# Squares behind the high parts, a raw tile of its own for the third down chunk, and block sums and squares moved into pass two, in a one-core decoder layer

## The reference

```python
def reference(x, ..., mlp_pre_g, w_up, w_down, mlp_post_g):
    ...
        h = h + rms_norm(mix @ w_out[l], attn_post_g[l])
        u = rms_norm(h, mlp_pre_g[l])
        a = jnp.square(jax.nn.relu(u @ w_up[l]))       # 1024 -> 4096
        h = h + rms_norm(a @ w_down[l], mlp_post_g[l]) # 4096 -> 1024
    return h
```

## Time and profile before

| what | value |
|---|---|
| median of 3 runs | 611.48 us (611.33 to 612.48) |
| the profiled execution's own time | 612.76 us |
| its span in the trace | 611.0 us |
| TensorE busy (matmuls) | 580.5 us, 95% |
| VectorE busy | 410.3 us, 67% |
| ScalarE busy | 310.6 us, 51% |
| GpSimd busy | 108.8 us, 18% |
| mean DMA rate | 166 GB/s |
| up stage, chunk 2 to the last | 276.57 to 440.83 us of the span |
| down product | 440.83 to 603.66 us |

### The profile page before, as it was taken

The page is one execution under the profiler, slowest core; times in us unless marked ns, Lnnn a source line. Parts: engine busy times, 40 slices in busy tenths (PEclk is TensorE's granted clock), DMA queues, the critical chain, the costliest instruction groups (busy, mean ns, idle before and its releaser), DMA issues.

```text
span 611.0 us, 8355 instructions
## 1 busy us (share of the span) xinstructions
PE 580.5 (95%) x2900; PEld 483.4 (79%) x2900; DVE 410.3 (67%) x787; ACT 310.6 (51%) x651; POOL 108.8 (18%) x165
## 2 busy tenths in 40 slices
PE   7999999999999999999999999999869999999995
PEld 7988898887787788997777777777748888888874
DVE  3448582788788408427657747757857897777797
ACT  5563262788898324544353352354324566555571
POOL 1153200346798101300000000000000000000034
PEclk9999999999999999999999999999998999999998
DMA  8441412000120082055877877777697555554503
GB/s 301 127 131 55 169 70 69 1 1 1 70 70 1 17 294 70 0 207 197 293 267 271 272 280 263 270 291 263 230 348 274 179 193 198 208 195 172 185 1 137
DMA packets 43777, 101.45 MB, mean 166 GB/s; under 512 B 3937, under 2 KB 22113, under 8 KB 39649
## 3 DMA queue, kind: packets, MB, share of 16 engines
q1 hardware_dynamic: 42704, 101.04, 46.9%
q10 hardware_dynamic: 1040, 0.00, 0.1%
HBM read 82.16 MB, written 18.87 MB: 165 GB/s over the span
## 4 chain that ended last, share of the span: by engine, by line
PE 59%; DVE 20%; ACT 10%; issue 5%; DMA 4%; DVEq 1%; SPq 0%; ACTq 0%; POOL 0%; POOLq 0%
PE bank L1188 19%; PE bank L1189 18%; PE bank L1190 18%; ACT w_hi L509 8%; DVE w_lo L797 6%; DVE stage L1083 5%; DVE relu L1062 3%; PE bank L1358 2%; DMA w_raw<-in_w_down 1%; DVE pT_lo L794 1%; ACT probs L621 1%; DVE bank L926 1%; DMA x_sb<-in_x 1%; DMA stage<-in_w_down 1%; DVE w_lo L794 1%
## 5 line engine op out<-in xcount | busy, mean ns | idle before, releaser
L1188 PE MATMUL bank<-uT_hi,w_hi 128*128 128x512 f32 (+1 forms) x280 | 105.5, 377 | 8.1 <-DVE w_lo L797 8.1
L1190 PE MATMUL bank<-uT_hi,w_lo 128*128 128x512 f32 (+1 forms) x280 | 103.9, 371 | 0.0
L1189 PE MATMUL bank<-uT_lo,w_hi 128*128 128x512 f32 (+1 forms) x280 | 103.9, 371 | 0.0
L509 ACT ACTIVATE w_hi<-w_raw 128x1024 fp32r<-128x1024 f32 (+2 forms) x65 | 62.7, 1010 | 72.4 <-PE bank L1190 63.8
L797 DVE SCALAR_TENSOR_TENSOR w_lo<-w_raw,g_up,w_hi 128x256 fp32r<-128x256 f32 x128 | 52.1, 481 | 66.9 <-ACT w_hi L509 66.9
L794 DVE TENSOR_TENSOR w_lo<-w_raw,w_hi 128x1024 fp32r<-128x1024 f32 (+1 forms) x57 | 67.8, 1232 | 40.8 <-ACT w_hi L509 40.6
L1188 PE MATMUL bank<-w_hi,a_hi 128*128 128x512 f32 x224 | 88.6, 396 | 6.9 <-DVE w_lo L794 6.9
L1189 PE MATMUL bank<-w_lo,a_hi 128*128 128x512 f32 x224 | 88.1, 393 | 0.0
L1190 PE MATMUL bank<-w_hi,a_lo 128*128 128x512 f32 x224 | 87.9, 392 | 0.0
L749 ACT ACTIVATE act_sb<-relu 128x512 f32 (+1 forms) x32 | 20.3, 635 | 106.1 <-DVE relu L1062 106.1
L1188 PEld LDWEIGHTS bank<-uT_hi,w_hi 128*128 128x128 f32 x280 | 52.7, 188 | 22.2 <-issue 13.5
(11 more groups left out here) (148 smaller groups left out, 1042.5 us busy)
## 6 DMA issues: line engine op xcount, KB each, us to landing
w_raw<-in_w_up SPq DMA_DIRECT2D x16, 1024.0 KB, 5.3
stage<-in_w_down SPq DMA_DIRECT2D x16, 1024.0 KB, 4.9
pair_sums<-stage SPq DMA_DIRECT2D x16, 1024.0 KB, 4.0
w_raw<-pair_sums SPq DMA_DIRECT2D x16, 1024.0 KB, 4.7
w_raw<-in_w_down SPq DMA_DIRECT2D x12, 1024.0 KB, 5.8
w_raw<-in_w_in SPq DMA_DIRECT2D x6, 1024.0 KB, 5.8
w_raw<-in_w_out SPq DMA_DIRECT2D x4, 1024.0 KB, 4.8
x_sb<-in_x SPq DMA_DIRECT2D x8, 256.0 KB, 6.0
```

What stands on the lines that cost most here:

```text
L509: return nc.scalar.activation(out, whole, ACT.Copy, scale=scale)
L1188: nc.tensor.matmul(out, lh, rh, start=start, stop=False)
L1189: nc.tensor.matmul(out, lh, rl, start=False, stop=False)
L1190: return nc.tensor.matmul(out, ll, rh, start=False, stop=stop)
```

## The change

Five things are changed; all of them are in the MLP.

1. ScalarE in the up stage makes the high parts of the next chunk first and squares the second bank of the chunk before only behind them (`activation(i, 2 * j - 1)`), then the first bank of the present chunk. The high and low parts of the first three activation chunks (`down_a_hi`, `down_a_lo`, c = 0 to 2) all come behind the loop.
2. `raw_more[0]`, the raw tile of d2, gets memory of its own; a placeholder keeps the old place. So d2's load waits for nothing and is issued before d1's.
3. The last pair (15) is no longer loaded, summed and stored in the up stage: chunk d23 loads its rows of `w_down` directly, and VectorE makes its four sums in place behind the low parts of d21 and d22 (`last_block_sums`).
4. The combinations after pass two are spread: those of `finish(0)` behind the low parts of d25, those of `finish(1)` and the last two behind the low parts of d26.
5. The squares and GpSimd's scaling of the first halves of tokens 0 and 1 (`c11`) move up from the end to d12; the squares of tokens 2 and 3 come behind the high parts of d27, and `scaled_y(2, 0)` behind the low parts of d27.

The diff, cut to its core:

```diff
-        raw_more = [sb(f"w_raw{i + 2}", [P, CW]) for i in range(2)]
+        raw_more = [None, sb("w_raw3", [P, CW])]
+        in_place_of_uT = sb("in_place_of_uT", [P, CW])
...
         stage += [sb("stage1", [P, CW])]
+        raw_more[0] = sb("w_raw2", [P, CW])
...
-                elif c < 4:
+                elif c == 3:
                     sp.wait_ge(up_full, NF)
-                else:
+                elif c > 3:
                     sp.wait_ge(dwl, c - 3)
...
-                    src, n = sums[q], 0
+                    src, n = (sums[q], 0) if q < N2 - 1 else (w_down_v[:, 2 * q:2 * q + 2, :], 2)
...
-            for j in range(2):
-                down_chunk(j)
-                next_sums(NF // 4, j)
-            for j in range(2):
-                sp.wait_ge(stage_sums, 4 * (NF // 2 + j - 1))
-                store_sums(j, NF // 2 + j - 2)
+            down_chunk(0)
+            next_sums(NF // 4, 0)
+            down_chunk(2)
+            down_chunk(1)
+            for j in (1, 0):
+                sp.wait_ge(stage_sums, 4 * (NF // 2 - 1 - j))
+                store_sums(j, NF // 2 - 2 - j)
...
+            def activation(i, tile):
+                act.wait_ge(relu_c, i * 4 + (tile + 1))
+                nc.scalar.activation(act_sb[:, bass.ds(i * 4 + tile, 1), :], relu[:, tile % 2:tile % 2 + 1, :],
+                                     ACT.Square).then_inc(a_ready, 1)
...
                             mlp_hi(1 - j, i * 2 + (UP_CH + j + 1))
-                    for m in range(2):
-                        if last and j == 1 and m == 1:
-                            down_w_hi(1)
-                        act.wait_ge(relu_c, i * 4 + (2 * j + m + 1))
-                        nc.scalar.activation(act_sb[:, bass.ds(i * 4 + (2 * j + m), 1), :], relu[:, m:m + 1, :],
-                                             ACT.Square).then_inc(a_ready, 1)
+                        activation(i, 2 * j - 1)
+                    activation(i, 2 * j)
...
             up_step(0, first=True)
-            down_a_hi(0)
             with act.Fori(1, NF // 4 - 1) as i:
                 up_step(i)
-            down_a_hi(1)
-            down_a_hi(2)
+            for c in range(3):
+                down_a_hi(c)
             up_step(NF // 4 - 1, last=True)
+            down_w_hi(1)
+            activation(NF // 4 - 1, 3)
...
-                if c == NDOWN - 2:
+                if c == N1 + 4:
                     act.wait_ge(stage_out[0], 16 * (NF // 4))
-                    for t in (2, 3):
-                        for b in range(2):
-                            y_square(t, b)
-            for b in range(2):
-                for t in range(2):
+                    for t in range(2):
+                        y_square(t, 0)
+            for t in (2, 3):
+                for b in range(2):
                     y_square(t, b)
+            for t in range(2):
+                y_square(t, 1)
...
-                            if last and j == 1:
-                                block_sums(i, j)
...
+            def last_block_sums(m0):
+
+                b11, b12, b21, b22 = (d_raw(N1 + N2 - 1)[:, TOP * q:TOP * q + TOP] for q in range(4))
+                sums = ((b11, b12, b11), (b12, b22, b12), (b22, b22, b11), (b21, b21, b22))
+                dve.wait_ge(*down_arrived(N1 + N2 - 1))
+                for m in (m0, m0 + 1):
+                    if m:
+                        dve.wait_ge(last_sums, m)
+                    nc.vector.tensor_tensor(*sums[m], ALU.subtract).then_inc(last_sums, 1)
...
-                    for t in range(2):
-                        dve.wait_ge(p_full, 5 + t)
-                        dve.wait_ge(comb, 3 + t)
-                        combine(ps[P7[t]][:, :], u3(t), ps[P5[t]][:, :])
-                        combine(u2(t), u2(t), ps[P5[t]][:, :])
-                if c == NDOWN - 1:
-                    dve.wait_ge(g_post_in, 32)
-                    dve.wait_ge(comb, 10)
-                    scaled_y(2, 0)
                 down_w_lo(c)
                 if c == N1 + N2 + 1:
+                    finish(0)
+                if c == N1 + N2 + 2:
+                    finish(1)
...
+                if c in (N1 + N2 - 3, N1 + N2 - 2):
+                    last_block_sums(2 * (c - N1 - N2 + 3))
```

More of the change, by code:

```diff
@@ L206, in build @@
         stage_in, stage_out = [[sem(f"stage{j}_{d}") for j in range(2)] for d in ("in", "out")]
-        stage_sums = sem("stage_sums")
+        stage_sums, last_sums = sem("stage_sums"), sem("last_sums")
         s3_ready, s2_ready, s1_ready, s4_ready = sem("s3_ready"), sem("s2_ready"), sem("s1_ready"), sem("s4_ready")
@@ L386, in down_chunk @@
                 sp.dma_start(dst, src).then_inc(down_arrived(c)[0], 16)
-            for j in range(2):
-                down_chunk(j)
-                next_sums(NF // 4, j)
-            for j in range(2):
-                sp.wait_ge(stage_sums, 4 * (NF // 2 + j - 1))
-                store_sums(j, NF // 2 + j - 2)
+            down_chunk(0)
[5 more added lines that the diff above has]
+                store_sums(j, NF // 2 - 2 - j)
             sp.wait_ge(y_s, 2 * NT)
             sp.dma_start(post_g[:, :], mlp_post_g.to_broadcast([P, D])).then_inc(g_post_in, 16)
-            for c in range(2, NDOWN):
+            for c in range(3, NDOWN):
                 if c == N1:
                     for j in range(2):
-                        sp.wait_ge(stage_out[j], 16 * (NF // 4))
+                        sp.wait_ge(stage_out[j], 16 * (NF // 4 - j))
                 down_chunk(c)
@@ L482, in _ @@
                 rms(4, t, D, h_sq(t))
-            rms(5, 2, D, 6 * NT + 2, parts=2)
-            rms(5, 3, D, 6 * NT + 4, parts=2)
             pool.wait_ge(g_post_in, 32)
             for t in range(2):
-                pool.wait_ge(sq, 6 * NT + 5 + t)
+                pool.wait_ge(sq, 6 * NT + 1 + t)
                 nc.gpsimd.tensor_tensor(c11[:, t, :], c11[:, t, :], post_g[:, 0:TOP], ALU.mult).then_inc(c11_scaled, 1)
+            rms(5, 2, D, 6 * NT + 4, parts=2)
+            rms(5, 3, D, 6 * NT + 6, parts=2)
             rms(5, 0, D, 6 * NT + 7, parts=2)
@@ L710, in down_w_hi @@
                 act.wait_ge(*down_arrived(c))
+                if c == N1 + N2 - 1:
+                    act.wait_ge(last_sums, 4)
                 if c == 1:
@@ L767, in _ @@
                     act.wait_ge(d_used, N1)
-                    act.wait_ge(stage_out[1], 16 * (NF // 4))
+                    act.wait_ge(stage_out[1], 16 * (NF // 4 - 1))
                     for t in range(2):
@@ L1102, in _ @@
             up_step(0, first=True)
-            down_a_lo(0)
             with dve.Fori(1, NF // 4 - 1) as i:
                 up_step(i)
-            down_a_lo(1)
-            down_a_lo(2)
+            for c in range(3):
+                down_a_lo(c)
             up_step(NF // 4 - 1, last=True)
@@ L1111, in combine, with finish @@
                 nc.vector.tensor_tensor(out, a, b, ALU.add).then_inc(comb, 1)
+            def finish(t):
+                dve.wait_ge(p_full, 5 + t)
+                dve.wait_ge(comb, 3 + t)
+                combine(ps[P7[t]][:, :], u3(t), ps[P5[t]][:, :])
+                combine(u2(t), u2(t), ps[P5[t]][:, :])
+            def last_block_sums(m0):
[6 more added lines that the diff above has]
+                    nc.vector.tensor_tensor(*sums[m], ALU.subtract).then_inc(last_sums, 1)
             def scaled_y(t, n):
@@ L1117, in scaled_y @@
                         dve.wait_ge(h_ready, 2 * NT + 2 * n - 1 + b)
-                    dve.wait_ge(sq, 6 * NT + 2 * n + b + 1)
+                    dve.wait_ge(sq, 6 * NT + 2 * n + b + 3)
                     nc.vector.tensor_tensor(un[:, w], y_half(t, b), post_g[:, w], ALU.mult).then_inc(y_s, 1)
@@ L1169, in _ @@
                     token_sum((c - 7) // 2, 4)
+            dve.wait_ge(g_post_in, 32)
+            dve.wait_ge(comb, 10)
+            scaled_y(2, 0)
             un_halves = [un[:, 0:TOP], un[:, TOP:]]
```

## The result

The changed kernel takes **596.19 us** (median of 4 runs, 595.35 to 597.10); the kernel before, run beside it, 611.98 us (611.33 to 612.76). The ratio is 0.9742, with a 95% interval of 0.9719 to 0.9765: faster by 15.8 us. The forecast was 590.0 us, with a range of 588.8 to 593.0. The direction is right; the time is outside the range, 6.2 us above the forecast. The profiled execution took 595.35 us, with a span of 593.5.

What follows compares the result with a forecast made beforehand. TensorE, nearly always busy, loses only gaps and slow-clock matmuls; a ScalarE-VectorE ring of 11.58 us paces the up stage. Gains 11.5 + 1.75 + 4.9 + 2.4 + 0.9 = 21.4 us, from 611.48 to 590.0 us; range 588.8 to 593.0.

Steps and rivals of the forecast that it cites:

- Squares behind the high parts: Up stage: low parts ready before TensorE is free, so TensorE sets the pace at 10.91 us a chunk; gain 11.5 us.
- the stage stays slow: Rival, up stage: something still ties high parts to the second relu, only 9.9 us gained, 601.6 us; chance 0.05.
- the clock falls under unbroken matmuls: Rival, up stage: without pauses the granted clock falls, up to 724 us if all 672 matmuls ran so; chance 0.02.
- that of the loop turns: Rival, up stage: TensorE's six loop turns show, 0.1 to 0.57 us each, 590.6 to 593.4 us; chance 0.14.
- SyncE's queue in this stage: ... Free: Up stage: loads and stores fit the new pace, store 4.0 us, 288 GB/s against 410 seen elsewhere; no cost.
- one of the signs of being wrong: Listed signs of a wrong forecast; the one meant is the clock at 0.5 anywhere after 276 us.
- Last pair away: End of up stage: without pair 15's sums d1's low parts are done before d0 ends; gain 1.65 + 0.10 = 1.75 us.
- Own tile: d2's load issued about 17 us before the up stage ends: gap of 4.9 us and slow clock of 2.4 us gone.
- Combinations: Ahead of d25: four combinations instead of eight before its low parts, so its gap goes; gain 0.80 + 0.10 = 0.9 us.
- d3: Rival, down product: d3's load, still bound to uT, comes late, costing 0.9 us, 590.9 us; chance 0.08.
- The end: After the last matmul: same instructions, no change; its rival has work slip past that matmul by a us or so, 591, chance 0.05.
- Early c11: d12 and d13: GpSimd's two scalings beside low parts slow VectorE by at most 2.7 us, covered by idle time; nothing.

Runs made afterwards that it cites:

- e2: Changed kernel with pair 0's block sums made a step earlier and SyncE's first turn written out, store ahead of the `w_up` load: 590.51 us, ratio 0.9657.
- f2: e2 with d2's raw tile back at its old place, its load issued with d3's: 591.66 us, ratio 0.9667.
- f1: Kernel before with the new order of squares (as e4) and the earlier first sums and SyncE turn of e2: 597.12 us, ratio 0.9753.
- f3: e2 with `finish(0)` and `finish(1)` ahead of d25's low parts again, as in the kernel before: 591.67 us, ratio 0.9669.
- f4: e2 with one disturbance: once, at chunk 6, SyncE waits for one chunk's low parts more before issuing the store: 599.78 us, ratio 0.9808.
- e4: Kernel before with only the new order of squares and the three first activation chunks behind the loop: 611.56 us, ratio 0.9999.
- e1: Changed kernel with d1's load issued before SyncE waits for the store of pair 12's sums: 594.52 us, ratio 0.9715.

## Why the prediction was right and wrong

- **Squares behind the high parts, 11.5 us: right for TensorE.** The stage ran without a gap, 10.88 us a chunk; d0 began 12.0 us earlier (the 11.5, 0.03 us more a chunk, and a start of the stage 0.1 us earlier). The rivals by which the stage stays slow or the clock falls under unbroken matmuls are gone (153.00 us busy, clock 1.00), and that of the loop turns too: the stage holds six of them, and its 672 matmuls, from 276.46 to 428.79, start 0.227 us apart on average and never more than 0.23. (The busy time of 153.00 us would not show it, as the modelled ends hide gaps up to 0.16 us; the starts do.) The Trainium skill, Advanced Engine Details and Errata, Control Flow Timing, has about 108 ns for a compare-and-branch; in this trace none of it shows between the matmuls.
- **"SyncE's queue in this stage: ... Free": the step that failed.** The reasoning took the store at its old 4.0 us, a time that had been measured with the transfers 3 to 4 us apart, and compared the bytes with a rate: 288 GB/s against 410. The rate was indeed below the 410: 273 GB/s in the stretch above. But what counts on a queue that waits for a landing is the time of that one store, and that depends on when the others are issued: 9.8 us (median) for 4.0. I left out that the pace of the stage and the turn of SyncE are nearly equal, so that one turn with the transfers together (10.5 for the store, 1.3 for the three issues) is longer than a chunk. The price: d1's load is issued at 423.7, where e2 issues it at 414.7, and costs 3.16 us of gap and 1.7 us of slow clock, 4.9 in this profile. No rival named a late load of d1, but one of the signs of being wrong came up, the clock at its lower level behind 276 us. e2, in which only the start of the stage differs, has 590.5 us for the 590.0 forecast. By the traces of before and e2 its gain is 11.9 us up to d0 (440.83 - 428.97), 10.1 from there to the last matmul and 0.2 behind it, 22.2 on the scale of the spans for the 21.4 of the sum; that the medians come out within 0.5 us of the forecast is in part luck, as two of the terms below (pair 15 and the own tile) miss by 5 to 6 us each and make up for each other.
- **Last pair away, 1.75 us: undersized.** The sums of pair 15 ahead of d1 are gone, but pair 15 did more harm than that. In the timeline of SyncE before, its load, sums and store hold the queue until d2's load goes out at 446.18, 5.4 us after d0's start at 440.83.
- **Own tile, 4.9 + 2.4 us: right in the sum, given to the wrong part.** With pair 15 gone, d2's load is issued 0.2 us after the stage's end even from the old place (428.91, d0 at 428.72), and f2 loses only 1.1 to 1.3 us. What part 3 is worth by itself was not run. f1 and f2 come nearest: both have the old place of the tile and the transfers apart, and from d0's first matmul to the last one they take 159.8 and 153.6 us. Less the 0.9 of the combinations, which f2 has and f1 has not, some 5 us go to pair 15 out of the way.
- **Combinations, 0.9 us:** right, 0.9 by f3's row. **d3:** no wait of TensorE for it in any kernel. **The end:** last matmul at 586.02, span 593.5, so 7.25 us behind its slot (586.02 + 0.23), where it was 7.51 before (611.0 - 603.26 - 0.23); the forecast had no change. The residual that took 1.84 us beside GpSimd takes 0.75 like the others.
- **Early c11, nothing:** right. VectorE's timeline in the chunk before and in the one beside GpSimd's two scalings (1.31 and 1.48 us, from 497.7):

```profile
491.71 1.02 DVE L804 TENSOR_TENSOR a_lo<-act_sb,a_hi 128x512 fp32r<-128x512 f32 x2
492.64 0.42 DVE L804 TENSOR_TENSOR a_lo<-s,a_hi 128x256 fp32r<-128x256 f32 x1
...
497.15 2.12 DVE L804 TENSOR_TENSOR a_lo<-act_sb,a_hi 128x512 fp32r<-128x512 f32 x2
499.19 1.52 DVE L804 TENSOR_TENSOR a_lo<-s,a_hi 128x256 fp32r<-128x256 f32 x1
```

The last two rows do what the first two do a chunk earlier and take 1.1 us more each, 2.2 for both scalings; the low parts that follow were in time.

What stays open: the four runs of the changed kernel lie two by two, at 595.4 and at 597.0, and those of e2 within 0.3 us. The first is in keeping with a lateness that piles up over 14 chunks, but I have a profile of a 595.35 run alone, so the cause is not shown; the mean granted clock was 0.995 in the first pair of runs and 0.990 in the second. How far each transfer slows which other one was not measured either, only the three together.

## What to carry to other kernels

When a stage gets faster, look at the engine that issues its transfers as at any other engine: list its turn with the waits for landings in it, and compare the turn, not the bytes, with the new pace. A transfer's time read from a trace holds for the spacing it had there. Where a queue waits for its own store, have the store issued apart from the loads, and see to the first turn, since a loop at the edge can keep either spacing, by how it starts (e2, f4). And part 1 alone would have measured as worthless (e4): before a part is thrown away, find what ate its gain.

## What the runs showed of the hardware that was not expected

- A 1 MB store takes 4.1 us (median) when it is issued 3.7 us behind one 1 MB load and the other load was issued 3 us before that one (e2). It takes 7.0 when it is issued 3.6 us behind two loads that are 0.65 us apart (the changed kernel, 287.26), and 9.8 to 10.5 when both loads, a pair's and a `w_up` chunk's, are issued in the 1.3 us before it; the `w_up` load goes from 5.3 to 8.1 us, the pair's load, which is first, stays at 4.9. The mean rate of the two kernels over a chunk is alike (279 GB/s in e2 from 381.6 to 392.5, 267 in the changed kernel from 376.1 to 387.9).
- The same loop ran in either of two spacings: stores of 4.1 us to the end of the stage (e2), or, after one store that came late, of about 10 to the end of it (f4).
- A gap of 1.15 us in TensorE left the clock at 1.00 (f2); behind one of 2.4 us (e1, ahead of d1) some eight matmuls ran at 1.2 GHz, behind one of 3.16 us (the changed kernel) nine. Ahead of these gaps TensorE had been busy without a break since 276 us. The length of the gap alone does not decide: in the kernel before, which had paused at every chunk, a gap of 2.4 us ahead of chunk 15 (427.15 to 429.82) left the clock at 1.00.
